# TensorE adds all gathered rows but one per stage in a two-layer trunk

## The reference

```
h = x
for layer in range(2):
    h = h + mixer[layer](rms_norm(h))
    h = h + peer(rms_norm(h))

# peer, per position and head (8 heads): the best 16 of 16,384 experts
q = x @ w_q
s1, s2 = q[:64] @ keys1, q[64:] @ keys2      # 128 scores each
e = best 16 of the sums of top16(s1) and top16(s2);  g = softmax(their scores)
a = gelu(u[e] . x) * g
out = sum over 8 heads x 16 experts of a * v[e]
```

## Time and profile before

| | us |
|---|---|
| median of three runs | 2,897.97 |
| the profiled execution | 2,902.58 |
| its span, first to last instruction | 2,900.4 |
| TensorE busy (matmuls) | 2,284.9 |
| VectorE busy | 2,184.6 |
| ScalarE busy | 1,183.7 |
| GpSimd busy | 1,244.1 |
| mean granted TensorE clock | 0.915 |

### The profile page before, as it was taken

How to read it: one execution, slowest core, us unless ns; L and a number is a source line. 1 busy time by engine, 2 the same in 40 slices (tenths; PEclk the granted TensorE clock), 3 DMA queues, 4 the chain that set the end, 5 groups by cost and what they waited for, 6 DMA issues and landing times.

```text
span 2900.4 us, 27200 instructions
## 1 busy us (share of the span) xinstructions
PE 2284.9 (79%) x7394; PEld 1213.3 (42%) x7394; DVE 2184.6 (75%) x5166; ACT 1183.7 (41%) x3457; POOL 1244.1 (43%) x1049
## 2 busy tenths in 40 slices
PE   9779787788877887786887878877788878886567
PEld 8536442454424554243443434443354434432122
DVE  2688678876878757796688876988679876887664
ACT  3154334344343443445344453435534453433333
POOL 0254335443444333444434543354434444345655
PEclk9899999899999898998899988989889998988989
DMA  6599999999999999999999999999999999999998
GB/s 271 209 418 421 398 398 416 421 421 403 415 420 421 420 375 420 420 418 421 421 393 406 422 421 420 389 416 421 421 402 406 421 421 421 399 421 421 422 422 350
DMA packets 170817, 1170.27 MB, mean 403 GB/s; under 512 B 19668, under 2 KB 19928, under 8 KB 36136
## 3 DMA queue, kind: packets, MB, share of 16 engines
q0 software_dynamic: 147456, 1073.81, 89.7%
q1 hardware_dynamic: 23208, 94.74, 8.3%
HBM read 1164.28 MB, written 4.19 MB: 403 GB/s over the span
## 4 chain that ended last, share of the span: by engine, by line
DMA 28%; DVE 14%; PE 11%; issue 6%; POOL 3%; ACT 3%; POOLq 0%; DVEq 0%; ACTq 0%
DMA ring<-in_uv,pick 26%; PE acc L1723 6%; DVE ring L1094 4%; POOL ring L666 3%; PE ps L1514 3%; DVE side L1085 1%; DMA xc<-h 1%; DMA stream<-in_strips 1%; ACT diag L1368 1%; DVE arena L969 1%; DVE arena L950 1%; DVE arena L1040 1%; DVE arena L1044 1%; DVE arena L951 1%; DVE arena L1031 1%
## 5 line engine op out<-in xcount | busy, mean ns | idle before, releaser
L666 POOL DMA_INDIRECT ring<-in_uv,pick x1024 | 1239.7, 1211 | 1630.5 <-PE acc L1723 1092.9
L1723 PE MATMUL acc<-ring,diag 128*128 128x512 f32 x2988 | 1542.5, 659 | 465.3 <-ACT diag L1368 462.3
L1094 DVE CUSTOM_DVE_ANT_0 ring<-ring,h_now 128x1024 f32<-128x1024 f32 x1024 | 1235.4, 1222 | 490.2 <-DMA ring<-in_uv,pick 474.0
L1723 PEld LDWEIGHTS acc<-ring,diag 128*128 128x128 f32 x2988 | 582.6, 207 | 1287.7 <-ACT diag L1368 702.8
L1357 ACT ACTIVATE gelu<-dots 128x1 f32<-128x1 f32 x1024 | 206.1, 201 | 1264.6 <-DVE dots L1094 1258.0
L1085 DVE SCALAR_TENSOR_TENSOR side<-ring,coef,side 128x1024 f32<-128x1024 f32 x270 | 346.0, 1281 | 23.1 <-ACT coef L1360 23.0
L1360 ACT ACTIVATE coef<-gate,gelu 128x1 f32<-128x1 f32 x1024 | 302.0, 295 | 33.2
L1368 ACT ACTIVATE diag<-ident,coef 128x128 f32<-128x128 f32 x747 | 300.1, 402 | 29.8 <-PE acc L1723 5.5
L1514 PE MATMUL ps<-resident,actT 128*128 128x256 f32 x896 | 220.3, 403 | 14.5 <-ACT actT L1169 14.5
L1514 PEld LDWEIGHTS ps<-resident,actT 128*128 128x128 f32 x896 | 178.1, 202 | 58.9 <-issue 18.2
L1481 PE MATMUL ps<-actT,stream 128*128 128x128 f32 x960 | 124.9, 291 | 23.6 <-DMA stream<-in_strips 22.7
(11 more groups left out here) (198 smaller groups left out, 1454.6 us busy)
## 6 DMA issues: line engine op xcount, KB each, us to landing
stream<-in_strips SPq DMA_DIRECT2D x102, 512.0 KB
resident<-in_strips SPq DMA_DIRECT2D x18, 1024.0 KB, 12.9
ring<-in_uv,pick POOLq DMA_INDIRECT x1024
ring<-in_strips SPq DMA_DIRECT2D x9, 1024.0 KB, 19.6
arena<-in_keys SPq DMA_DIRECT2D x8, 512.0 KB
xc<-in_x SPq DMA_DIRECT2D x4, 512.0 KB
h<-arena SPq DMA_DIRECT2D x4, 512.0 KB, 11.4
xc<-h SPq DMA_DIRECT2D x4, 512.0 KB
```

What stands on the lines that cost most here:

```text
L666: pool.indirect_dma_start(ring[:, n % SLOTS, :], None, tables[layer], bass.IndirectOffsetOnAxis(ap=pick[:, col:col + 1], axis=0),).then_in ...
L1094: dve.tensor_tensor_reduce(ring[:, slot, 0:D], ring[:, slot, 0:D], h_now[:], 1.0, 0.0, ALU.mult, ALU.add, dots[:, slot:slot + 1]).then_inc ...
L1723: m = pe.matmul(acc[:, b * 512:(b + 1) * 512], diag[:, turn % 4, :], ring[:, slot, D + b * 512:D + (b + 1) * 512], start=(r == 0 and i == ...
```

## The change

The table VECTOR is rewritten: VectorE keeps one add per stage, pick 4 of round 2 in stage 0 and pick 1 of round 0 in all others, which is the one that takes the residual in. TENSOR, the turns, the diagonals, the fold's wait and the release of slots are worked out from the table by code that stays as it is.

```diff
 VECTOR = {
-    "first": (
-        ((),) * 2 + ((4,),) + ((),) + ((1, 4, 7),) + ((0, 2, 4, 6),) + ((1, 3, 5, 7),) * 2 +
-        ((0, 2, 4, 6),) * 3 + ((1, 4, 7),) + ((2, 6),) + ((),) * 3),
-    "gla": (
-        ((1, 4, 7),) * 3 + ((0, 2, 4, 6),) + ((1, 4, 7),) * 2 + ((0, 2, 4, 6),) + ((1, 3, 5, 7),) +
-        ((0, 3, 6),) + ((2, 6),) + ((1, 4),) + ((2, 6),) + ((4,),) + ((),) * 3),
-    "swa": (
-        ((1, 4, 7),) * 2 + ((0, 2, 4, 6),) + ((0, 4),) + ((1, 5),) + ((0, 3, 6),) + ((2, 6),) +
-        ((1, 4, 7),) * 2 + ((2, 6),) + ((1, 3, 5, 7),) + ((0, 3, 6),) + ((),) * 4),
+    "first": ((),) * 2 + ((4,),) + ((),) * 13,
+    "gla": ((1,),) + ((),) * 15,
+    "swa": ((1,),) + ((),) * 15,
 }
```

## The result

The changed kernel takes 2,959.6 us (median of four runs, 2,949.3 to 2,964.8) against 2,898.0 (four runs): a ratio of 1.0207, 95% interval 1.0181 to 1.0234. That is some 60 us slower, where +26 was forecast.

The account below looks back on a forecast made before the run. The prediction took the gather transfers as the bound; local crowding on TensorE summed to +30 us, the clock gave back 4, so +26 on the profiled 2,902.6, stated as 2,924 us for the runs' median, range 2,896 to 2,967.

Parts of the forecast that it names:

- The ring of diagonals: ScalarE's four diagonals span four picks instead of six to eight, so it runs less far ahead; taken at nothing.
- all absorbed: Rival: stream waits and the ring take all added turns, the clock repays the remaining 4 us; 2,898 us, 14%.
- faster: Rival: the fuller TensorE keeps its clock and strips behind stream waits shrink; 2,887 us, 10%.
- the heavy one: Rival: nothing is hidden and each lateness is passed on in full; +75 us, 2,973 us, 16%.
- long stretches under 400 GB/s in stages 3 to 6: Sign of being wrong, for rounds 1 to 4 of these stages: the ring would have no 8 us.
- the terms of stages 0 to 2: Costs of crowded strips and picks: 7 us in stage 0, 4 in stage 1, 3 in stage 2.
- 340 to 380: Stage 0 behind its pinch: four adds, 6.9 us against 10.0 idle, mostly stream waits; hides its own, pays back little.
- the stream waits behind it absorb some: Stage 1, 600 to 640 us: late by 9.1, bounds 1 and 9; partly absorbed, taken at 4 us.
- the ring's 8 us: The gather slots let TensorE be some 8 us late before a transfer is lost, less where other work holds it.
- The query strips: Stages 3 to 6, after four query strips: 7 adds, late by 7.3 us; ring full, taken at 1 each.
- the choice of experts: Stages 3 to 6, before this choice: 4 adds, late by 4.7 us ahead of a dip; taken at 3 each.
- The clock: A fuller TensorE runs some strips in stages 0 to 2 at full speed: 4 us back, bounds 0 and 15.

Follow-up runs that it names:

- pe_time_only: Kernel before with all VectorE adds kept, plus four zero-matrix passes on TensorE at each of the 269 moved picks' places: 2,946.7 us, 1.0162.
- direct_ring8: direct_ring4 with eight diagonals in the ring instead of four, in the space of side: 2,940.6 us, 1.0136 to the kernel before.
- gla_rounds_8_12: Kernel before with only the 20 adds of rounds 8 to 12 of stages 1 and 2 moved to TensorE: 1.0034.
- only_gla: Kernel before with only the table row of stages 1 and 2 changed, 72 adds moved to TensorE: 2,915.7 us, 1.0062.
- direct_ring4: Changed kernel with all 1,024 picks on TensorE and the residual added straight from xc, side dropped: 2,934.5 us, 1.0118 to the kernel before.
- pe_time_half: pe_time_only with two zero passes instead of four for each of the 269 picks: 2,903.6 us, 1.0018 to the kernel before.
- gla_rounds_0_5: Kernel before with only the 36 adds of rounds 0 to 5 of stages 1 and 2 moved to TensorE: 1.0003.
- direct_swa_tensor: Kernel before with the residual straight from xc into TensorE's accumulator and all picks of stages 3 to 7 on TensorE: 2,901.5 us, 1.0008.

## Why the prediction came out as it did

**Right.** The bound, the transfers, and the direction of the mechanism: TensorE's added time (48 of 60 us in pe_time_only), felt locally where strips and picks crowd, free in stage 7 (-1.3 us). VectorE's relief was worth nothing (+287 us of waits for 317 of work removed). The ring of diagonals, taken at nothing though ScalarE's wait for it rose from 5.5 to 192.6 us, was worth nothing (direct_ring8). Of the rivals, all absorbed and faster are out. The time lies between the forecast and the heavy one (+75), and stages 0 to 2 came out near the heavy rival's terms (16.3, 17.5 and 6.2 against 11, 9 and 6), stages 3 to 6 far from them (17.3 against 48). One of the prediction's own signs of being wrong appeared: long stretches under 400 GB/s in stages 3 to 6, here 389 and 399 in the 80 us shown above for stage 4. A small slip, on which nothing hangs: the add that the fold waits for is twelve rounds old in stage 0 only, fourteen in the others.

**Wrong: the terms of stages 0 to 2.** They came to 14 and measured 40, of which some 7 go with a stretch at a lower clock (under Open). Two steps made them small.

The first is "340 to 380: 4 adds = 6.9 against 10.0 idle, mostly waits for streamed strips, so this pinch hides its own", and its kin in stage 1, "the stream waits behind it absorb some". gla_rounds_8_12 moves adds in such rounds alone and pays 10 us, in its profile all of it in stage 1: the turns between two waits found cover there, the turns ahead of them didn't, and strips behind the waits ran at the lower clock. The forecast looked at the 80 us and the 40 us ahead of a pinch and left out the rest of it. Taken over the whole crowded part, one stretch a stage, the kernel before shows, all work and then the adds of line 1085 alone:

```profile
220.00:380.00 160.00, 131.32 (x495) 84.72 (x494) 106.80 (x166) 59.01 (x167) 62.17 (x51) 0.90 1.00 408
560.00:740.00 180.00, 147.40 (x550) 89.46 (x551) 123.08 (x205) 72.46 (x209) 73.14 (x62) 0.96 1.01 411
920.00:1100.00 180.00, 147.52 (x521) 89.64 (x520) 120.25 (x201) 72.26 (x207) 69.42 (x59) 0.93 0.99 402
```

```profile
220.00:380.00 160.00, 32.05 (x25) 0.90 1.00 408
560.00:740.00 180.00, 29.98 (x24) 0.96 1.01 411
920.00:1100.00 180.00, 29.34 (x23) 0.93 0.99 402
```

In stage 0, 25 adds of 1.72 us are 43.0 against 28.7 idle, 14.3 late, and 16.3 were measured. In stage 1 24 are 41.3 against 32.6, 8.7 late, measured 10.1 where that entry moved alone. In stage 2 23 are 39.6 against 32.5, 7.1 late, measured 6.2. The measured figures of stages 0 and 2 are the changed kernel's, that of stage 1 isn't: the changed kernel grew by 17.5 us there, and only_gla by 3.1 in stage 2. In pe_time_only the three stages grew by 16.1, 9.7 and 6.1 us, in direct_ring4 by 19.0, 9.5 and 7.0.

The second is the ring's 8 us, subtracted in stage 0 and counted as cover for the rest ("less the ring's 8 the loss is 3; with nothing hidden 11. ... I take 7"). The sums just made hide nothing and come near in these three stages, so no cover by the ring shows in them. The same rule gives pe_time_half: at 0.86 us an add the three stretches have 21.5, 20.6 and 19.8 us to place in 28.7, 32.6 and 32.5 idle, none late, and the four query-strip stretches 6.0 in 4.7, late by 1.3 each; 5 us were measured. That agrees in size only: in its profile stages 3 to 6 didn't grow, and stages 0 and 1 grew by 1.5 and 2.5. It gives gla_rounds_0_5 too: 480 to 612 us has 30.1 idle for 18 adds, 31.0 us, and nothing was measured. This rule was formed after the result, its stretches were chosen then, and those two kernels weren't made to test it.

In two other places it fails. The first line is stage 4 of the kernel before around its query strips, the second the same for line 1085 alone, the third rounds 8 to 12 of stage 1:

```profile
1580.00:1820.00 240.00, 197.22 (x640) 107.56 (x640) 184.94 (x360) 108.85 (x321) 110.58 (x93) 0.91 1.01 419
```

```profile
1580.00:1820.00 240.00, 41.01 (x32) 0.91 1.01 419
```

```profile
660.00:770.00 110.00, 89.63 (x346) 50.48 (x344) 76.84 (x204) 43.40 (x129) 44.93 (x38) 0.98 1.00 405
```

In stage 4, 32 adds are 55.0 us against 42.8 idle, 12.2 late, and 5.0 were measured; with the ring's 8 us taken off, 4.2 would be left. In stage 1, ten adds are 17.2 us against 20.4 idle, none late, and gla_rounds_8_12 grew by 8.9 us there. So what is shown is that the terms of stages 0 to 2 were made small by cover that wasn't there. Whether the ring covers some lateness elsewhere stays open.

**Right by its sum, wrong in its places: stages 3 to 6.** The sum, 16 us against 17.3, was luck. The query strips were put at 1 us ("the ring is full there") and the choice of experts at 3. The windows above show the opposite. In 1642 to 1722 the transfers miss (422 - 389) / 421 x 40 = 3.1 and (421 - 399) / 421 x 40 = 2.1 us, together most of the stage's 5. At the dip in front of the choice of experts the answer to before's 373 GB/s is no lower:

```profile
1842.00:1882.00 40.00, 34.72 (x157) 20.89 (x156) 29.40 (x99) 16.23 (x40) 15.24 (x13) 0.96 1.00 410
```

With full lateness at the strips and none at the choice, the prediction's own terms sum to 11.2 + 9.1 + 6.2 + 4 x 7.3 = 55.7, against 55.5: a fit made afterwards, and good as a sum only; direct_swa_tensor has the same strips with as many turns among them, and none of its stages 3 to 6 is more than 0.5 us longer than before. Stage 0 grew by 5 us more than that and stage 1 by 8, stages 3 to 6 by 3 us less each.

**The clock.** As a mean its direction was right; what it gave back can't be told, and in stage 1's pinch it fell, as shown above and under Open. The mean granted clock rose from 0.915 to 0.966. As a mixture of the levels 1.2 and 2.4 GHz the lower one held for 2 x 0.085 x 2,900 = 493 us before and 2 x 0.034 x 2,956 = 201 after, and a pass fell from 659 to 616 ns. The Trainium skill (TensorE: Matmul & The Clock Gate, section on the clock gate) has sustained activity lift the throttle; the trace agrees with that as a mean, and the rule's result, a sum 11 us lower, didn't come, since the time lies with the transfers: stage 7 gained 1.3 us at 0.98. The forecast of TensorE's busy time, over 2,650 us, missed for this reason: 4,064 passes at 616 ns overlapped to 1,901.9 us, and the total stayed at 2,606.7.

**Open.** Thirteen us lie between pe_time_only and the changed kernel, 7.8 of them in stage 1 of the profiles. The traces show the place, 230 to 260 us into the stage and the 30 us behind it, in the changed kernel and in only_gla:

```profile
725.90:755.90 30.00, 26.89 (x61) 13.42 (x60) 8.63 (x19) 7.66 (x19) 5.26 (x6) 0.77 0.83 316
755.90:785.90 30.00, 27.51 (x129) 16.35 (x128) 21.10 (x79) 10.10 (x34) 12.73 (x11) 1.00 0.96 377
```

```profile
708.30:738.30 30.00, 26.28 (x99) 14.95 (x98) 13.24 (x26) 11.36 (x30) 9.28 (x8) 1.00 0.97 368
738.30:768.30 30.00, 27.24 (x129) 16.05 (x128) 21.48 (x82) 10.99 (x32) 10.96 (x10) 1.00 1.01 419
```

At 0.77 five picks' passes took 10.96 us against 8.85, and one strip half 3.78 against 1.99. Over the 60 us the transfers miss 10.6 us against 3.9; in pe_time_only and direct_ring4, with clocks of 1.00 and 0.94 in the first half, they miss 3.4 and 3.9. So some 7 us go with a stretch at a lower clock in the one execution that was profiled. Why the clock fell there, and whether it does in every execution, isn't shown. only_gla, in which TensorE also releases all slots there, grew by 10.1 us in that stage and not by 17.5, so it isn't the releases by themselves. direct_ring4 lacks it as well. The changed kernel's own runs lie 16 us apart. The remaining five us weren't traced.

## What to carry to other kernels

To cost work that moves onto an engine which feeds a saturated queue, take the whole crowded stretch of each stage and not only its tightest part, and set the added time against the engine's idle time in it. Here that came near in three stages and failed in two other places, so it gives a size and not a figure. Don't take two kinds of cover off the sum, a ring's slack and waits, unless a row shows each. Idle time that hangs on the engine's own progress (a single-buffered stream) can be used up sooner than it looks, and half of an added load may be nearly free where the whole is not. Spread what is moved by place: here 36 adds in the first six rounds of two stages cost nothing, and 20 in five later rounds 10 us. And look for a wait at the start of a stage that the engine used to make up in its idle time: with the direct residual nearly the same turns in stages 3 to 7 cost 3.4 us instead of 17.7.

## What was not expected of the hardware

231 us of added matmul time cost 5 us and 463 us cost 48: between them TensorE's busy share in the tightest stretch went from 73.2 to 76.5 of 80 us and the transfers from 419 to 376 GB/s. A mean clock of 0.962 in place of 0.915 came with no gain that could be measured (direct_swa_tensor, 1.0008 [0.9998, 1.0019]). And a gather's issue on GpSimd got hardly shorter when 269 of VectorE's adds went: the median is 940 ns against 975, the mean 1,247 against 1,211.
